# Two gates of a two-block layer on one core: thin products over side-by-side pieces, and single-pass products over stacked pieces

## The reference

```python
log_f = jax.nn.log_sigmoid(fg_logit + b_f)
cum = jnp.cumsum(log_f, axis=1)
logits = einsum('bqhd,bkhd->bhqk', qb, k) * scale
logits = logits + cb[..., None] - cum_k[:, :, None, :]
```

```python
hn = rmsnorm(h, mixer_norm)
gk = jnp.einsum('btzr,zrd->zbtd', lr, w_gate_up) + b_gate[:, None, None, :]
logdec = jax.nn.log_sigmoid(gk) / GLA_GATE_NORM
```

## Time and profile before

| | before |
|---|---|
| median of 3 runs (lowest, highest) | 1723.49 us (1722.32, 1723.55) |
| the profiled execution: time, span | 1725.12 us, 1723.4 us |
| mean granted TensorE clock | 0.996 |
| TensorE products busy | 1701.1 us (99%) |
| DVE, ACT, POOL busy | 1024.5 (59%), 802.2 (47%), 100.7 us (6%) |
| weight units of 512 KB loaded | 572 |
| DMA, mean | 183 GB/s |

### The profile page before, as it was taken

One profiled execution on the slowest core, in us unless ns is written; L12 is line 12 of the kernel. 1 busy time (PEld: TensorE's weight loads), 2 busy tenths in 40 slices (PEclk: granted clock), 3 DMA queues, 4 the chain that ended last, 5 costly groups with the idle time before them and its releaser, 6 DMA issues.

```text
span 1723.4 us, 21669 instructions
## 1 busy us (share of the span) xinstructions
PE 1701.1 (99%) x7790; PEld 1399.6 (81%) x7790; DVE 1024.5 (59%) x1084; ACT 802.2 (47%) x967; POOL 100.7 (6%) x90
## 2 busy tenths in 40 slices
PE   8999999999999999999999999999999999999997
PEld 6888877888777888877888888888888888888886
DVE  4544465566655799955554555555465465565755
ACT  4534444443457555545544443443434434434553
POOL 6000000000110122200000000000000000000001
PEclk9999999999999999999999999999999999999999
DMA  8566655666464545555666666666666666666564
GB/s 264 172 184 184 184 147 144 219 220 208 134 211 136 170 146 159 159 159 182 209 194 185 192 187 194 189 189 195 186 191 193 186 191 191 189 188 194 178 187 131
DMA packets 158976, 315.46 MB, mean 183 GB/s; under 512 B 9665, under 2 KB 9665, under 8 KB 158017
## 3 DMA queue, kind: packets, MB, share of 16 engines
q1 hardware_dynamic: 157456, 304.12, 59.0%
q0 software_dynamic: 1456, 10.46, 1.6%
HBM read 310.36 MB, written 4.19 MB: 183 GB/s over the span
## 4 chain that ended last, share of the span: by engine, by line
PE 97%; DVE 1%; issue 0%; ACT 0%; DMA 0%; POOL 0%; POOLq 0%; SPq 0%; DVEq 0%
PE acc L580 30%; PE acc L582 30%; PE acc L581 30%; PE aux L596 2%; PE aux L736 2%; PE aux L802 0%; PE aux L640 0%; PE aux L750 0%; PE aux L749 0%; PE aux L639 0%; DMA w_raw<-in_w_in 0%; DVE h_tok L1472 0%; PE aux L720 0%; DVE w_lo L1242 0%; PE aux L627 0%
## 5 line engine op out<-in xcount | busy, mean ns | idle before, releaser
L1242 DVE TENSOR_TENSOR w_lo<-w_raw,w_hi 128x1024 fp32r<-128x1024 f32 x572 | 705.1, 1236 | 588.6 <-ACT w_hi L928 588.2
L928 ACT CAST w_hi<-w_raw 128x1024 fp32r<-128x1024 f32 x572 | 600.2, 1051 | 829.0 <-PE acc L582 804.7
L580 PE MATMUL acc<-w_hi,a_hi 128*128 128x512 f32 x1660 | 655.9, 395 | 2.2 <-DVE w_lo L1242 2.2
L582 PE MATMUL acc<-w_hi,a_lo 128*128 128x512 f32 x1660 | 648.5, 391 | 0.0
L581 PE MATMUL acc<-w_lo,a_hi 128*128 128x512 f32 x1660 | 647.8, 390 | 0.0
L580 PEld LDWEIGHTS acc<-w_hi,a_hi 128*128 128x128 f32 x1660 | 312.7, 188 | 71.0 <-issue 8.6
L582 PEld LDWEIGHTS acc<-w_hi,a_lo 128*128 128x128 f32 x1660 | 312.4, 188 | 65.6
L581 PEld LDWEIGHTS acc<-w_lo,a_hi 128*128 128x128 f32 x1660 | 312.8, 188 | 62.9 <-issue 0.2
L580 PE MATMUL acc<-w_hi,act_hi 128*128 128x512 f32 x320 | 124.7, 390 | 0.0
L582 PE MATMUL acc<-w_hi,act_lo 128*128 128x512 f32 x320 | 124.6, 389 | 0.0
L581 PE MATMUL acc<-w_lo,act_hi 128*128 128x512 f32 x320 | 124.6, 389 | 0.0
(11 more groups left out here) (232 smaller groups left out, 889.3 us busy)
## 6 DMA issues: line engine op xcount, KB each, us to landing
w_raw<-in_ffn_w_in SPq DMA_DIRECT2D x176, 512.0 KB, 3.7
w_raw<-in_w_in SPq DMA_DIRECT2D x112, 512.0 KB, 3.7
w_raw<-in_gla_w_in SPq DMA_DIRECT2D x96, 512.0 KB, 3.8
w_raw<-in_ffn_w_out SPq DMA_DIRECT2D x88, 512.0 KB, 3.9
w_raw<-in_w_out SPq DMA_DIRECT2D x32, 512.0 KB, 4.5
w_raw<-in_gla_w_out SPq DMA_DIRECT2D x32, 512.0 KB, 4.5
w_raw<-in_ple_w_gate SPq DMA_DIRECT2D x32, 512.0 KB, 4.4
x_raw<-in_x_cols SPq DMA_DIRECT2D x8, 256.0 KB, 7.8
```

The costliest lines, as they stand in the source:

```text
L580: pe.matmul(banks[t][:], hi[:, k + c, tok], wh, start=st, stop=False)
L582: mm = pe.matmul(banks[t][:], lo[:, k + c, tok], wh, start=False, stop=en)
L928: nc.scalar.copy(w_hi[u % RING][:], w_raw[u % RING][:]).then_inc(hi_done, 1)
L1242: nc.vector.tensor_tensor(w_lo[u % RING][:], w_raw[u % RING][:], w_hi[u % RING][:], ALU.subtract).then_inc(lo_done, 1)
```

## The change

Both thin jobs: high and low pieces lie side by side in one tile (fg_two, lr_two). The product with the tokens' high part runs over both at once, the one with the tokens' low part over the high pieces only, so two products per chunk stand where three stood. The halves come out in different rows and are added by a plain f32 product with a 0/1 matrix (fg_fold, lr_fold). For the forget gate that is a new job, fgt, at (1, 3), whose result has the 8 sums at rows 0 and 32 of 128; the log-sigmoid and sum then run over 128 rows. ACT's steps move to (1, 5), DVE's to (1, 6), ci to (2, 3). For the second gate it takes the place of the turn at g = 10.

The 0/1 product of the scores and the gate products become single-pass: their operands are high and low pieces stacked over 128 rows (ncum: high at rows 0 to 7, low at 32 to 39, all other rows of sel are 0; gate_two: high, high, low, low against high, low, high, low of the tokens in lr_four). The product with sel runs once over all 384 columns and ahead of the two q-k products. The gate weights are loaded four times over, by 8 DMAs, cast and subtracted at g = 6. The gate's bias leaves the product and becomes a column of vec, which DVE and ACT add, in two pieces of 256 columns where one of 512 stood. sel is built later in POOL's queue.

The core of the diff:

```diff
-V_CONV, V_PS, V_MIX, V_ON, V_FFN, V_PLE, NVEC = 0, 12, 16, 32, 36, 52, 68
+V_CONV, V_PS, V_MIX, V_ON, V_FFN, V_PLE, V_BG, NVEC = 0, 12, 16, 32, 36, 52, 68, 84
...
-            if (p, j) == (1, 6):
+            if (p, j) == (1, 3):
+                order.append(("fgt", 0))
+            if (p, j) == (2, 3):
                 order.append(("ci", 0))
...
-    gate_up = at("gate_up", [2 * RANK + 1, 2, GH * GDK], F32, 104 * KB)
+    gate_raw = at("gate_raw", [P, 2, GH * GDK], F32, 96 * KB)
+    gate_two = at("gate_two", [P, 2, GH * GDK], F32R, 104 * KB)
...
-    sel = at("sel", [NH, NH, P], F32, W + 55 * KB)
+    sel = at("sel", [P, NH, P], F32R, W + 55 * KB)
...
-    lr_hi = at("lr_hi", [P, KD, 2 * RANK], F32R, W + 58 * KB)
-    lr_lo = at("lr_lo", [P, KD, 2 * RANK], F32R, W + 60 * KB)
-    lrt = at("lrt", [P, TT, 2 * RANK + 1], F32, W + 64 * KB)
-    lrT = at("lrT", [2 * RANK + 1, TOK], F32, W + 64 * KB + 288)
-    restart = at("restart", [P, TOK + 1], F32, W + 65 * KB + 288)
+    lr_two = at("lr_two", [P, KD, 4 * RANK], F32R, W + 58 * KB)
+    lr_flat = at("lr_flat", [4 * RANK, TOK], F32, W + 62 * KB)
+    lr_rows = at("lr_rows", [P, TT, P], F32, W + 63 * KB)
+    lr_four = at("lr_four", [P, TOK], F32R, W + 64 * KB)
...
-            pool.dma_start(bf_col[:], b_f[0].rearrange("(h a) -> h a", a=1)).then_inc(vec_in, 16)
+            nc.gpsimd.memset(bf_col[:], 0.0).then_inc(bf_clear, 1)
+            pool.wait_ge(bf_clear, 1)
+            for r in (0, ROW2):
+                pool.dma_start(bf_col[r:r + NH, :], b_f[0].rearrange("(h a) -> h a", a=1)).then_inc(bf_in, 16)
...
+            nc.gpsimd.memset(sel[:].bitcast(F32), 0.0).then_inc(sel_built, 1)
+            for i, r in enumerate((0, ROW2)):
+                pool.wait_ge(sel_built, i + 1)
+                nc.gpsimd.affine_select(sel[:], sel[:], [[-1, NH], [0, P]], ALU.not_equal, 1.0, base=-r,
+                                        channel_multiplier=1).then_inc(sel_built, 1)
...
-            nc.gpsimd.memset(gate_up[:], 0.0).then_inc(up_clear, 1)
+            nc.gpsimd.memset(gate_raw[:], 0.0).then_inc(up_clear, 1)
             pool.wait_ge(up_clear, 1)
-            for z in range(2):
-                pool.dma_start(gate_up[z * RANK:(z + 1) * RANK, z, :], gla_w_gate_up[0, z]).then_inc(up_in, 16)
-                pool.dma_start(gate_up[2 * RANK:2 * RANK + 1, z, :], gla_b_gate[0, z:z + 1, :]).then_inc(up_in, 16)
+            for r in range(0, P, 2 * RANK):
+                for z in range(2):
+                    pool.dma_start(gate_raw[r + z * RANK:r + (z + 1) * RANK, z, :], gla_w_gate_up[0, z]).then_inc(up_in, 16)
...
-            def thin(name, hi, lo, n):
-
-                o = begin(name)[0:n, 0:TOK]
+            def thin_two(name, two, n):
+
+                o = begin(name)[0:2 * n, 0:TOK]
                 for k in range(KD):
-                    pe.matmul(o, hi[:, k, :], a_hi[:, k, :], start=k == 0, stop=False)
-                    pe.matmul(o, lo[:, k, :], a_hi[:, k, :], start=False, stop=False)
-                    mm = pe.matmul(o, hi[:, k, :], a_lo[:, k, :], start=False, stop=k == KD - 1)
+                    if k == 0:
+                        pe.matmul(o, two[:, k, :], a_hi[:, k, :], start=True, stop=False)
+                    pe.matmul(o[0:n, :], two[:, k, 0:n], a_lo[:, k, :], start=False, stop=False)
+                    if k:
+                        mm = pe.matmul(o, two[:, k, :], a_hi[:, k, :], start=False, stop=k == KD - 1)
                 mm.then_inc(aux_done, 1)
 
             def scores(h):
 
                 if h == 0:
                     pe.wait_ge(fg_neg, 1)
+                    pe.wait_ge(sel_built, 3)
                 b = begin("s", h)
+                pe.matmul(b[:, 0:P + TOK], sel[:, h, :], ncum[:], start=True, stop=False)
                 for c, n, q in ((0, P, 0), (P, TOK, P)):
-                    o = b[:, c:c + n]
-                    pe.matmul(o, qT[:, h, q:q + P], kT[:, h, 0:n], start=True, stop=False)
-                    mm = pe.matmul(o, sel[:, h, :], ncum[:, 0:n], start=False, stop=True)
+                    mm = pe.matmul(b[:, c:c + n], qT[:, h, q:q + P], kT[:, h, 0:n], start=False, stop=c == P)
...
+                    if (p, j) == (1, 3):
+                        job_read(pe, "fg")
+                        b = begin("fgt")
+                        pe.matmul(b[:, 0:TOK], fg_fold[:], fg_flat[:], start=True, stop=True).then_inc(aux_done, 1)
+                    if (p, j) == (2, 3):
...
+                        pe.wait_ge(fold_lr, 1)
                         b = begin("lr_tok")
                         for t in range(TT):
-                            mm = pe.transpose(b[:, t * 2 * RANK:(t + 1) * 2 * RANK], lrT[0:2 * RANK, t * P:(t + 1) * P],
-                                              ident[0:2 * RANK, 0:2 * RANK])
+                            mm = pe.matmul(b[:, t * 2 * RANK:(t + 1) * 2 * RANK], lr_flat[:, t * P:(t + 1) * P], lr_fold[:],
+                                           start=True, stop=True)
                         mm.then_inc(aux_done, 1)
                     if name == "lrt":
                         job_read(pe, "lr_tok")
                         b = begin("lrt")
                         for t in range(TT):
-                            mm = pe.transpose(b[0:2 * RANK + 1, t * P:(t + 1) * P], lrt[:, t, :], ident[:])
+                            mm = pe.transpose(b[:, t * P:(t + 1) * P], lr_rows[:, t, :], ident[:])
...
-                            pe.wait_ge(up_in, 64)
+                            pe.wait_ge(up_split, 1)
                         b = begin("gk", i)
                         for k in range(2):
                             blk = 2 * (i % 4) + k
-                            mm = pe.matmul(b[:, k * TOK:(k + 1) * TOK], gate_up[:, i // 4, blk * P:(blk + 1) * P],
-                                           lrT[:], start=True, stop=True)
+                            mm = pe.matmul(b[:, k * TOK:(k + 1) * TOK], gate_two[:, i // 4, blk * P:(blk + 1) * P],
+                                           lr_four[:], start=True, stop=True)
...
+                if g == 6:
+                    act.wait_ge(up_in, 8 * 16)
+                    nc.scalar.copy(gate_two[:], gate_raw[:]).then_inc(up_hi_done, 1)
                 if g == 8:
                     job_done(act, "lr")
-                    nc.scalar.copy(lrT[0:2 * RANK, :], bank_of("lr")[0:2 * RANK, 0:TOK]).then_inc(read_of("lr"), 1)
+                    nc.scalar.copy(lr_flat[:], bank_of("lr")[0:4 * RANK, 0:TOK]).then_inc(read_of("lr"), 1)
...
+                    twice = [P, 2, 2 * RANK]
                     for t in range(TT):
-                        last = nc.scalar.activation(lrt[:, t, 0:2 * RANK],
-                                                    bank_of("lr_tok")[:, t * 2 * RANK:(t + 1) * 2 * RANK],
-                                                    ACT.Copy, scale=rstd[1][:, t:t + 1])
-                    last.then_inc(read_of("lr_tok"), 1)
+                        hi = lr_rows[:, t, :].bitcast(F32R).rearrange("p (a b r) -> p a b r", a=2, b=2)[:, :, 0, :]
+                        src = bank_of("lr_tok")[:, t * 2 * RANK:(t + 1) * 2 * RANK].rearrange(
+                            "p (a r) -> p a r", a=1).broadcast_to(twice)
+                        last = nc.scalar.activation(hi, src, ACT.Copy, scale=rstd[1][:, t:t + 1])
+                    last.then_inc(lr_rows_hi, 1)
                 if g == 12:
                     job_done(act, "lrt")
-                    nc.scalar.copy(lrT[:], bank_of("lrt")[0:2 * RANK + 1, 0:TOK]).then_inc(read_of("lrt"), 1)
+                    nc.scalar.copy(lr_four[:], bank_of("lrt")[:, 0:TOK]).then_inc(read_of("lrt"), 1)
...
-                        nc.scalar.activation(e, bank_of("gk", i)[:], ACT.Abs).then_inc(read_of("gk", i), 1)
+                        for k in range(2):
+                            col = V_BG + 2 * i + k
+                            last = nc.scalar.activation(e[:, k * TOK:(k + 1) * TOK],
+                                                        bank_of("gk", i)[:, k * TOK:(k + 1) * TOK], ACT.Abs,
+                                                        bias=vec[:, col:col + 1])
+                        last.then_inc(read_of("gk", i), 1)
...
+                        for r in (0, ROW2):
+                            nc.vector.tensor_tensor(fg_fold[:, r:r + NH], ident[0:2 * NH, 0:NH],
+                                                    ident[0:2 * NH, NH:2 * NH], ALU.add)
                         job_done(dve, "fg")
-                        nc.vector.tensor_scalar(fgz[:], bank_of("fg")[0:NH, 0:TOK], bf_col[:], None, ALU.add).then_inc(read_of("fg"), 1)
+                        nc.vector.tensor_copy(fg_flat[:], bank_of("fg")[0:2 * NH, 0:TOK]).then_inc(read_of("fg"), 1)
                     if (p, j) == (1, 4):
+
+                        dve.wait_ge(bf_in, 2 * 16)
+                        dve.wait_ge(vec_in, 16)
+                        job_done(dve, "fgt")
```

(39 more changed lines are left out.)

72 lines of the change are left out of this document (39 added, 33 removed).

## The result

The changed kernel takes 1703.55 us (median of 4, 1703.27 to 1703.85), the kernel before 1722.94 beside it (median of 4): a ratio of 0.9885, 95% interval 0.9874 to 0.9897.

What follows compares the result with a forecast made beforehand. TensorE's queue was taken to bound the kernel. Terms -3.7 - 8.9 - 8.3 + 1.05 = -19.9 us took the median from 1723.49 to 1703.6; with 0.5 for a short wait 1704.1, range 1702 to 1711.

Steps and rivals of the forecast that it cites:

- What bounds the kernel: TensorE, busy 1701.1 of 1723.4 us: each microsecond out of its queue comes off the span while weights keep ahead.
- Thin products: Both gates' thin jobs: 48 products become 32 at 0.117 us each, saving 1.87 us per job, -3.7 together.
- Sum spreading: Scores of eight heads: one single-pass product replaces the 8-row f32 ones, 2.09 to 0.98 us per head, -8.9 us.
- my bound of -9.6: Scores of eight heads: largest saving expected, in us, with the short q-k product at 0.22.
- Gate products: Eight gate jobs: two single-pass 128-row products replace 33-row f32 ones, 1.27 to 0.23 us per job, -8.3 us.
- Folds: Products adding the gates' halves: +0.7 us for the forget gate's, +0.3 for the second gate's, which replaces two transposes.
- A short wait: 0.5 us added to the forecast time for a brief wait of TensorE.
- The bounds: Limits on the sum of all terms on TensorE: between -14.7 and -20.7 us.
- Rival 1: Weights late in the gate stretch, near unit 25: one TensorE wait gives 1707.5 us, two 1711; chance 0.20.
- Rival 2: Single-pass gate and spreading products no cheaper than f32 ones; only thin products gain, 1720.8 us; chance 0.04.
- Rival 3: Weight loads of 16 gate and 8 spreading products exposed: 4.4 us given back, 1708.5 us; chance 0.05.
- Rival 4: Gate weights' DMAs land late, ACT's queue stands and TensorE stalls: slower, 1727 us or more; chance 0.03.

Runs made afterwards that it cites:

- 2 x 2 table: Changed kernel with gate products in f32 or single pass, 33 or 128 rows: jobs 1.27, 0.87 (f32), 0.64, 0.25 us; likewise scores, 8 or 128 rows: 2.09, 1.32, 1.63, 0.90.

## Why the prediction was right, and where it was off

**What bounds the kernel.** Right. TensorE's busy time fell by 21.7 us and the span by 21.3; no microsecond of the gain was lost to a wait.

**Thin products, -3.7.** Measured -3.6: the first job fell from 5.61 to 3.72 us, the second from 5.46 to 3.74. The forecast took the first job's 0.117 a product for both, but the second job's products before stood 0.114 apart, so it had less to give. Doubling a product brought 5.58 back.

**Sum spreading, -8.9.** Measured 8 x (2.09 - 0.84) = -10.0. The mechanism held, the size was off in one piece: I priced the q-k pair at 0.31 + 0.39 + 0.11 with its exit, and it took 0.46 + 0.19. More than half of that lies in the short product. The long product behind it starts at 202.14:

```profile
202.14 0.60 PE L656 MATMUL aux<-kT,qT 128*128 128x256 f32 x2
```

so the short product takes 0.22, where my 0.31 came from a row in which an 8-row product follows and held the change of height. The long one with its exit took 0.43 in place of 0.50. The sel product, 0.17 forecast, took 0.18. Even my bound of -9.6, which had the 0.22, was too small.

**Gate products, -8.3.** Measured -8.2. Four passes in place of one account for 0.62 of the 1.02 us per job and the height for 0.40. Single pass alone would have saved 5.0 us in eight jobs; the rest is the height, which the row of the old loads with its 0.35 idle already showed. The estimate by the Trainium skill (FP8 and Floating Point Precision, TensorE Precision Notes) was 5.7: near enough for the passes, and silent on the height.

**Folds, +0.7 and +0.3.** Measured +0.83 and +0.32. Both were priced from few-row products, as they were; at full height they are 0.45 and 0.45, and the turn that the second replaced took 0.44, so it would add nothing.

**A short wait, +0.5.** It did not come. The sum of the terms as measured is -3.6 - 10.0 - 8.2 + 1.15 = -20.65, against -19.9 forecast; 0.5 more came off before the first thin job, where TensorE starts at the lower clock in both traces and stays there for fewer products in the second. The profiled pair moved by 21.3 and the medians by 19.4, since the profiled execution of before lies 2.2 above its median. So the terms were 0.75 too small, the 0.5 for a wait made the forecast smaller still, and the medians moved by less than the terms as measured. That the forecast lies within 0.5 us of the median is partly luck. The bounds, too, do not add up: with +1.05 for the added work the prediction's own terms give -15.0 and -20.6, not -14.7 and -20.7, and the measured -20.65 lies at their edge.

**Rival 1, weights late.** It did not decide, but its arithmetic did: 1 us of margin forecast, 0.7 read, and 1.9 us of extra ACT work in that place made a wait of 1.0 and one of 0.4, while five units earlier it made none. The clock did not fall behind those, as I had it for such a wait; they were shorter than the one in the earlier trace rows. The 1.4 us for the six slow products was also too much: it took the difference of durations (0.63 and 0.39), which overlap, where start to start a slow product takes 0.43 and not 0.227, so 6 x 0.2 = 1.2.

**Rival 2, single pass no cheaper.** Refuted by the 2 x 2 table.

**Rival 3, loads exposed.** Refuted for the change: its full-height loads lie beside products and the gate job is 0.25 us, not 0.45. The rule in the Trainium skill (TensorE: Matmul & The Clock Gate, The mechanism), by which a load overlaps running products only where the row groups differ, does not fit these traces: a load starts under the running product where both have the same height, 128 rows or 33, and so share every row, and does not where the height changes, down or up.

**Rival 4, gate_raw late.** Refuted: the last landing is some 7 us ahead of the cast.

## What to carry to other kernels

Where TensorE is the bound, read a small job's price edge to edge, from the last large product before it to the second one after it, since part of it lies in the slow step at its exit. A product with few rows between full-height ones cost 0.15 to 0.4 us more here than the same at full height, about 0.2 for each change of height; padding its operands to 128 rows with zeros removes that. Stacking high and low pieces in the empty rows carries both in a single pass with no more time on TensorE; here it cost ACT 1.9 us and DVE 2.3 for the weights. How near the result is to that of plain f32 was not measured. Before filling a second engine to over 90% of a stretch, compute the margin of the ring at its worst point: here 0.7 us was left of 3.5.

## What the runs showed of the hardware that was not expected

The height of a product's weights has a price of its own, nearly independent of its passes: 0.40 us per gate job (33 rows), 0.75 per head (8 rows twice), 0.38 and 0.31 for the folds (16 and 64 rows). In the rows it is an idle load queue, up to 0.35 us, before the few-row load. It is the change of height that counts, down and up alike, and not the few rows in themselves. Inside a gate job of four f32 records with 33 rows the last two steps are 0.216 us, as at full height (0.215), while entry and exit are each 0.2 dearer; a scores job, with four changes, pays 0.73 to 0.77. Only the exit from 64 rows was cheaper, 0.1.

The layer norm's stretch, the same code in twelve kernels, took between 35.5 and 38.4 us at equal waits, by how many products ran at the lower clock behind each. Which kernel or run gets which is open. A few tenths of a per cent between single runs therefore say nothing here (runs of the kernel before lay between 1721.48 and 1725.67 in one series), and jobs were compared by their rows.
